# Second mixer of a two-layer diffusion backbone: copies shared out anew, the residual loaded late, and identity products on TensorE while the accumulators are loaded

## The reference, cut to what matters

```
u  = modulate(rms_norm(x), shift, scale)           # latents and context, 64 groups of 16 features
for d in (forward, backward):
    h[t] = lam_bar * h[t-1] + b_bar @ u[t]         # 64 complex states per group; context first, then latents
    y   += real(c_mat @ h)
z  = gelu(y + u * d_skip)
x  = x + gate * (val * sigmoid(gt)),   [val, gt] = z @ glu_w + glu_b
```

## Time and profile before

| what | us |
|---|---|
| median of three runs | 2512.29 (2508.5 to 2512.55) |
| the profiled execution, its time | 2506.16 |
| its span in the trace | 2504.4 |
| PE busy | 2143.6 (86% of the span) |
| DVE busy | 1092.3 (44%) |
| ACT busy | 509.8 (20%) |
| `s5_mixer`, from its first DMA to its last addition | 1461.3 to 1759.3 |

### The profile page before, as it was taken

How to read it: one execution, slowest core, us unless ns; L and a number is a source line. 1 busy time by engine, 2 the same in 40 slices (tenths; PEclk the granted TensorE clock), 3 DMA queues, 4 the chain that set the end, 5 groups by cost and what they waited for, 6 DMA issues and landing times. The chain is left out here.

```text
span 2504.4 us, 40476 instructions
## 1 busy us (share of the span) xinstructions
PE 2143.6 (86%) x11989; PEld 1189.9 (48%) x11990; DVE 1092.3 (44%) x2311; ACT 509.8 (20%) x945; POOL 433.9 (17%) x359
## 2 busy tenths in 40 slices
PE   5889999997999999999999816699789999988874
PEld 3765444744544444444444405354444444444442
DVE  8853365944543333333333338942532222222222
ACT  3443233611121111111111125220221111100000
POOL 1000000002012222222222210000122222232332
PEclk9999999998999999999999968799799999999997
DMA  9971002003799999999999669830499999899996
GB/s 358 386 265 46 34 34 84 1 1 131 264 346 355 354 358 357 359 351 350 355 358 358 202 158 329 275 146 0 160 404 375 361 363 358 274 390 372 385 385 207
DMA packets 173622, 666.72 MB, mean 266 GB/s; under 512 B 37666, under 2 KB 48898, under 8 KB 129882
## 3 DMA queue, kind: packets, MB, share of 16 engines
q1 hardware_dynamic: 121410, 564.71, 58.7%
q0 software_dynamic: 36160, 64.84, 11.0%
q10 hardware_dynamic: 15960, 35.96, 4.1%
HBM read 617.29 MB, written 86.09 MB: 281 GB/s over the span
## 5 line engine op out<-in xcount | busy, mean ns | idle before, releaser
L1518 PE MATMUL banks_l<-slotw_l,xTw_l 128*128 128x512 f32 x800 | 358.2, 601 | 27.7 <-issue 27.7
L1529 PE MATMUL banks_l<-slotn_l,xTn_l 128*64 128x256 f32 x2816 | 325.0, 383 | 34.5 <-issue 34.5
L1529 PEld LDWEIGHTS banks_l<-slotn_l,xTn_l 128*64 128x64 f32 x2816 | 212.0, 137 | 178.9 <-issue 104.8
L1518 PEld LDWEIGHTS banks_l<-slotw_l,xTw_l 128*128 128x128 f32 x800 | 148.5, 191 | 239.3 <-issue 239.3
L1568 PE MATMUL banks_l<-slotn_l,late_l 128*64 128x512 f32 x704 | 189.9, 615 | 19.6 <-DVE late_l L1356 17.9
L1547 PE MATMUL banks_l<-slotw_l,late_l 128*128 128x512 f32 x400 | 191.8, 602 | 15.4 <-DVE late_l L1338 15.4
L977 POOL DMA_INDIRECT xgw_l<-moe_h,idxw_l x58 | 60.6, 1045 | 741.0 <-PE banks_l L1463 367.1
L1005 POOL DMA_INDIRECT moe_acc<-late_l,idxn_l x88 | 151.2, 1718 | 190.5 <-DMA moe_acc<-late_l,idxn_l 172.5
L937 POOL IOTA slotw_l<- 128x1 f32 x2 | 0.3, 140 | 729.1 <-POOLq L69 431.3
L1335 DVE TENSOR_TENSOR late_l<-late_l,banks_l 128x256 f32<-128x256 f32 x50 | 21.0, 421 | 240.2 <-ACT late_l L1107 240.2
L556 PE MATMUL ps_a<-W_a,hT_a 128*128 128x512 f32 x288 | 124.9, 595 | 0.0
(11 more groups left out here) (433 smaller groups left out, 3235.0 us busy)
## 6 DMA issues: line engine op xcount, KB each, us to landing
slotn_l<-in_exp_w_gate SPq DMA_DIRECT2D x88, 1024.0 KB
slotn_l<-in_exp_w_up SPq DMA_DIRECT2D x88, 1024.0 KB
slotn_l<-in_exp_w_down SPq DMA_DIRECT2D x88, 1024.0 KB, 12.1
slotw_l<-in_exp_w_gate SPq DMA_DIRECT2D x50, 1024.0 KB
slotw_l<-in_exp_w_up SPq DMA_DIRECT2D x50, 1024.0 KB
slotw_l<-in_exp_w_down SPq DMA_DIRECT2D x50, 1024.0 KB
w_p<-in_mod_w SPq DMA_DIRECT2D x12, 2048.0 KB, 15.4
W_a<-in_ar_w_in SPq DMA_DIRECT2D x5, 2048.0 KB, 9.4
```

The source lines that it names most:

```text
L1518: last = pe.matmul(pGU_w, xT_w[b % 2][:, k, :], wgu[0][b % WIDE_RING][:, :, k, :], start=(k == 0), stop=(k == KD - 1))
L1529: last = pe.matmul(pGU_n[H * side:H * side + H, b % 2], xT_n[b % 2][:, k % 4, H * (k // 4):H * (k // 4) + H], w[:, :, k, P * side:P * side ...
```

## The change

- ACT issues the loads of `vec` ahead of all its others.
- PE multiplies the identity by itself 90 times (128 x 128, into the bank 6 that nobody reads) after it has transposed the modulation vectors (L2452) and before it waits for `Xn`.
- The eight copies of the residual go. `x` is loaded from the first accumulator and `XR` (the lower half of `XS`) from the second, by eight DMAs each, late: the first between the GLU's bias and the second half of its weights, the second when the last product of the output stage is done. DVE adds them behind the first GLU tile.
- So SP issues the factors of half-blocks 4 to 6 at once. ACT issues the first modulation weight when `Xn` is complete, the next two after uT. The weights' buffers are rotated, and output factors 3 and 4 wait for m5 instead of m7.
- DVE makes its copy in half-blocks 2, 5, 8, 11 and 14 only, ahead of the sweep of the block that they belong to; ACT makes it in the other eleven. Sweeps are no longer interleaved with copies by thirds: `sweep(0)` follows half-block 1. PE's wait ahead of t0 counts all copies, as before.
- 57 memsets for 50.

```diff
-        w = [v.rearrange("p (k n) -> p k n", k=HK) for v in (ZU[:, 0], ZU[:, 1], XS[:, SG * NCL:])]
+        w = [v.rearrange("p (k n) -> p k n", k=HK) for v in (XS[:, SG * NCL:], ZU[:, 0], ZU[:, 1])]
+        XR = XS[:, 0:NL * D].rearrange("p (m d) -> p m d", m=NL)
...
-        XN_DVE, R_ACT = 5, 2
+        XN_DVE, R_ACT, WARM = 5, 2, 90
+        DVE_CTX = (2, 5, 8, 11, 14)
+        def evicted(hb):
+            return 3 * (hb + 1) - ctx_copied(hb)
+        def ctx_copied(hb):
+            return sum(k <= hb for k in DVE_CTX)
...
             for hb in range(R_ACT, NHB):
-                if hb == 4:
-                    sp.wait_ge(S['x_sum'], SL)
-                    for m in range(NL):
-                        for hh in range(2):
-                            sp.dma_start(x[hh * 64:hh * 64 + 64, m, :], X[0:64, 2 * m + hh, :]).then_inc(S['xres_in'], 16)
...
-            sp.wait_ge(S['mod_mm'], LATE)
+            sp.wait_ge(S['mod_mm'], LATE - 2)
...
+            for m in range(NL):
+                for hh in range(2):
+                    sp.dma_start(x[hh * 64:hh * 64 + 64, m, :], tile_rows(parts[0], m, hh)).then_inc(S['xres_in'], 16)
             glu_half(1)
+            sp.wait_ge(S['o_mm'], NB)
+            for m in range(NL):
+                for hh in range(2):
+                    sp.dma_start(XR[hh * 64:hh * 64 + 64, m, :], tile_rows(parts[1], m, hh)).then_inc(S['xres_in'], 16)
...
         def _(act):
+            [the three loads of vec, moved here from behind the loop]
             for j in range(2):
...
+            act.wait_ge(S['xn_done'], XN_DVE)
+            act.wait_ge(S['xn_act'], SL - XN_DVE)
+            act.dma_start(w[0], mod_weights(io, *MOD_LATE[0], 0)).then_inc(m_in[0], 16)
...
-            act.wait_ge(S['xres_in'], 16 * 8)
-            for n in range(3):
+            for n in range(1, 3):
                 act.dma_start(w[n], mod_weights(io, *MOD_LATE[n // 2], n % 2)).then_inc(m_in[n], 16)
...
+                if hb not in DVE_CTX:
+                    act.activation(VH[64:P, 0:NCC, :, gs].rearrange("p c a g -> p g a c"), v_of(hb)[64:P, :, :, 0:NCC], ACT.Copy)\
+                       .then_inc(S['va_done'], 1)
...
-            dve.wait_ge(S['xres_in'], 16 * 8)
-            for hb in range(NHB):
-                dve.wait_ge(S['va_done'], 2 * hb + 1)
-                dve.tensor_copy(VH[64:P, 0:NCC, ...], v_of(hb)[64:P, :, :, 0:NCC]).then_inc(S['vd_done'], 1)
-                if 2 <= hb < 14:
-                    b, third = divmod(hb - 2, 3)
-                    sweep(b, third)
-                    if third == 2:
-                        sweep(b, 3)
-            for b in range(4, NB):
+            dve.wait_ge(S['xn_act'], SL - XN_DVE)
+            for b in range(NB):
+                for hb in (2 * b, 2 * b + 1):
+                    if hb in DVE_CTX:
+                        dve.wait_ge(S['va_done'], evicted(hb - 1) + 1)
+                        dve.tensor_copy(VH[64:P, 0:NCC, ...], v_of(hb)[64:P, :, :, 0:NCC]).then_inc(S['vd_done'], 1)
                 for stage in range(4):
                     sweep(b, stage)
...
-            for _ in range(50):
+            for _ in range(57):
...
+                if u == 0:
+                    dve.wait_ge(S['xres_in'], 16 * 16)
+                    for t in range(NL):
+                        done(dve.tensor_tensor(x[:, t, :], x[:, t, :], XR[:, t, :], ALU.add))
+                    done.wait()
                 done(dve.tensor_tensor(x[:, m, c], x[:, m, c], a, ALU.add))
...
             last.then_inc(S['vec_mm'], 1)
+            for _ in range(WARM):
+                pe.matmul(ps[:, 6 * 512:6 * 512 + P], ident[:], ident[:], start=True, stop=True)
             pe.wait_ge(S['xn_done'], XN_DVE)
...
-            pe.wait_ge(S['va_done'], 2 * NHB)
-            pe.wait_ge(S['vd_done'], NHB)
+            pe.wait_ge(S['va_done'], evicted(NHB - 1))
+            pe.wait_ge(S['vd_done'], ctx_copied(NHB - 1))
```

More of the change, by code:

```diff
@@ L2087, in s5_mixer, with tile_rows @@
         NPAIR, NFILL = NCK // 2 - 1, NCL // 2
-        XN_DVE, R_ACT = 5, 2
+        XN_DVE, R_ACT, WARM = 5, 2, 90
[4 more added lines that the diff above has]
+            return sum(k <= hb for k in DVE_CTX)
+        def tile_rows(part, m, hh):
+            return part.rearrange("(m h c) d -> m h c d", m=NL, h=2)[m, hh, 0:NCL, :]
         CTX_OPS, STEPS = 4 * 4, NCL // 2 - 1
@@ L2178, in _ @@
         def _(act):
+            for s in range(2):
+                act.dma_start(vec[:, 2 * s:2 * s + 2], io['modrow'][1, s, 0:2 * D].rearrange("(a g j) -> g a j", a=2, j=SI)).then_inc(S['vec_in'], 16)
+            act.dma_start(vec[:, 4], io['norm1_g'][1].rearrange("(g j) -> g j", j=SI)).then_inc(S['vec_in'], 16)
             for j in range(2):
@@ L2181, in _ @@
                    .then_inc(x_in[j], 16)
-            for s in range(2):
-                act.dma_start(vec[:, 2 * s:2 * s + 2], io['modrow'][1, s, 0:2 * D].rearrange("(a g j) -> g a j", a=2, j=SI)).then_inc(S['vec_in'], 16)
-            act.dma_start(vec[:, 4], io['norm1_g'][1].rearrange("(g j) -> g j", j=SI)).then_inc(S['vec_in'], 16)
             act.dma_start(lam[:, 0].rearrange("p a b g -> p (a b g)"), io['s5_l8']).then_inc(S['l8_in'], 16)
@@ L2334, in sweep @@
                         dve.wait_ge(S['up'], n)
-                    dve.wait_ge(S['va_done'], 4 * (b + 1))
-                    dve.wait_ge(S['vd_done'], 2 * (b + 1))
+                    dve.wait_ge(S['va_done'], evicted(2 * b + 1))
+                    if ctx_copied(2 * b + 1):
+                        dve.wait_ge(S['vd_done'], ctx_copied(2 * b + 1))
                     dve.tensor_tensor(a, even, factor(0, 0, NPAIR, g), ALU.mult).then_inc(S['up'], 1)
@@ L2345, in sweep @@
                     dve.tensor_tensor(odd, a, c[:, :, ::-1, :], ALU.add).then_inc(S['up'], 1)
-            dve.wait_ge(S['xres_in'], 16 * 8)
-            for hb in range(NHB):
-                dve.wait_ge(S['va_done'], 2 * hb + 1)
-                dve.tensor_copy(VH[64:P, 0:NCC, :, 4 * hb:4 * hb + 4].rearrange("p c a g -> p g a c"), v_of(hb)[64:P, :, :, 0:NCC])\
-                   .then_inc(S['vd_done'], 1)
-                if 2 <= hb < 14:
-                    b, third = divmod(hb - 2, 3)
-                    sweep(b, third)
-                    if third == 2:
-                        sweep(b, 3)
-            for b in range(4, NB):
+            dve.wait_ge(S['xn_act'], SL - XN_DVE)
[3 more added lines that the diff above has]
+                        dve.wait_ge(S['va_done'], evicted(hb - 1) + 1)
+                        dve.tensor_copy(VH[64:P, 0:NCC, :, 4 * hb:4 * hb + 4].rearrange("p c a g -> p g a c"), v_of(hb)[64:P, :, :, 0:NCC])\
+                           .then_inc(S['vd_done'], 1)
                 for stage in range(4):
@@ L2472, in _ @@
                 if hb >= 4:
-                    pe.wait_ge(S['va_done'], 2 * (hb - 3))
-                    pe.wait_ge(S['vd_done'], hb - 3)
+                    pe.wait_ge(S['va_done'], evicted(hb - 4))
+                    if ctx_copied(hb - 4):
+                        pe.wait_ge(S['vd_done'], ctx_copied(hb - 4))
                 for g in range(4):
```

## The result

The change costs a quarter of a per cent. In 20 runs of each kernel the median after is 2512.18 us (2508.0 to 2524.86), before 2505.24 (2501.54 to 2516.3); the ratio is 1.0026 with a 95% interval of 1.0015 to 1.0037. The kernel before measured 7 lower over these 20 runs than in the first three of them, so the forecast of 2510.0 lies close to 2512.18 by its number, yet its sign is wrong: a gain of 2.3 was forecast, a loss of about 6.9 was measured.

A forecast was written before the change was run, and what follows sets the result against it. DVE's recurrence and the queue of weights and tables bound the mixer side by side, DVE's path longer by 2.8 us. First GLU product 2.3 earlier: 2506.16 - 2.3 = 2503.9 profiled, 2510.0 against the median; range 2503.0 to 2516.0.

The forecast's parts named there:

- the slack between m7 and the fill: Before the first fill, DVE was ready 2.8 us after m7 ended; afterwards the fill would wait for m7, not DVE.
- the start: Mixer's start up to V: X1's last part shares the engines with factors 4 to 6; last `sums` some 0.6 late.
- the estimate of equal turns: X1's last part at the start: queues served in equal turns would give a landing at up to 1497.2.
- X1's first part is issued 2 us later, so `sums(0)` about 1472.4: Start, loads of `vec` moved ahead: `sums(0)` about 1472.4, and PE starts the 90 products at 1476.9.
- It costs nothing: PE's 90 products ahead of uT: the block ends at 1498.9 to 1501.0, before `Xn` at 1502.0.
- copies and sweeps: During and after V: first sweep at T + 7.4, sweeps end at T + 39.9, saving DVE 7.6 us.
- ACT needs about 1.7 a half-block: ACT's copies in V: about 1.7 a half-block, 3.4 a block, so DVE stays the slower.
- I take 7.0: it lands at 1564.1: Weights' chain: weight 3, in an empty queue, takes 7.0 and lands at 1564.1 against 1564.8; m7 ends at 1602.9.
- the output stage: First fill to GLU: fill 3.4 earlier, block 5 only 0.7, first GLU product 2.3 earlier, within 0.7 to 3.4.
- The rival in which DVE's path decides: First fill: starts when DVE is ready, 1598.0, GLU 8.4 earlier at 1637.2; 2503.9; chance 28%.
- the GLU: GLU stage: loads of x and XR and four additions of 1.2 on DVE are hidden; nothing taken, 4.9 if uncovered.
- 7 more memsets, 0.9 us, lie ahead of the first tile [...] I take nothing.: DVE ahead of the first GLU tile: 7 more memsets, 0.9 us, are hidden and cost nothing.

The follow-up runs named there:

- held factors: Kernel after, but SP holds factors 4 to 6 until the last `sums`, as before; 2512.0 us, ratio 1.0025 against the kernel before.
- old copies: Kernel after, but DVE makes all 16 small copies, with sweeps interleaved by thirds as before; 2508.75 us, ratio 1.0002.
- factors first: Kernel after, but output factors 5 to 7 are issued ahead of the GLU's bias and first half of its weights; 2512.16 us, ratio 1.0005.
- the old ones: Kernel after with factors 4 to 6 held, copies and sweeps in the old order, and 46 memsets; 2508.57 us, ratio 1.0002.
- tables first: Kernel after, but SP issues table n-1 ahead of the wait for m(n-3) and weight n; 2517.04 us, ratio 1.0032.

## Why the prediction was wrong, by its steps

The GLU begins 8.5 later from the mixer's start. By the table of marks: V +3.6; t0 behind V +3.5; t0 and m0 at the lower clock +2.1; the chain from m0 to m7 -1.1; the slack between m7 and the fill -2.6; from the fill to the GLU +3.0. The forecast had, in this order, -0.8, +3.2, +2.4, -5.5, -2.7, +1.1. The first, fourth and last are wrong. The first and last had been taken towards the favourable end of their bounds, the fourth in the middle of its own (7.0 between 5.4 and 8.4). Together they make up 10.7 of the 10.8 between forecast and marks.

- **Failed: the start.** "Shared, it lands at 1489.2 + 4.9 = 1494.1, and `sums` starts some 0.6 late." It is 4.2 late by the marks; the bound was 4.0. The step took the third part's 4.9 us as the price of sharing, but SP's queue was running dry then; with 1.5 MB more behind it X1 shares to the end. The kernel with held factors shows this cause: there the last `sums` is back at 32.8. Here the estimate of equal turns, worked out from the round robin by packets of the Trainium skill ("DMA: Bandwidth & Descriptors", "Queues, rings and completion order"), which I set aside, was nearly right: a landing at 1497.2 is 35.9 in the marks' terms, and the last part landed at 1469.6 + 32.1 - 1465.34 = 36.4.
- **Failed: "X1's first part is issued 2 us later, so `sums(0)` about 1472.4".** It began at 18.5, not 11.1: issued behind the vectors, the first part took 16.3 to land. By itself that costs the last `sums` little (32.8 with held factors, for 32.3), but PE's products stand behind `sums(0)`, and so "It costs nothing" fell with it. Their length was right (22.6 for 22.0 to 24.1), the place wasn't (they began at 22.7 for 15.6); the 1.3 they bring is right too.
- **Right in the main: copies and sweeps.** First sweep 7.3 after V (7.4), sweeps' end at V + 40.1 (39.9), t0 at V + 36.5 (36.2), t0 and m0 5.4 (5.7), with the clock at 0.50 until 1564 and m0's end at 1565.5. The reading that t0 would fall behind DVE's copy of 14 was the change's centre, and with old copies it is back at V + 32.5. What was mis-sized is ACT: "ACT needs about 1.7 a half-block" was 1.92, since a half-block with three copies takes it 2.15 to 2.20 and one with two some 1.34: the third adds over 0.8, not 0.45. DVE stayed the slower, so t0 was not hurt by this, but about half of the delay stays when DVE's copy no longer is the last.
- **Failed: "I take 7.0: it lands at 1564.1".** Weight 3 took 9.7, above even the 8.4 of weight 0. The queue was empty, and the step took that for more of a gain than it was: of the 17 kernels five had 11.8 to 12.5 here, the one before among them, and twelve 8.9 to 10.1, none 7.0. Why a weight in an empty queue takes that long stays open. In the whole chain the loss of 2.7 at the landing and 1.6 behind it (36.9 for 35.3) turned 45.8 from m0's end to m7's end into 50.2. It had been 51.3: a chain whose length behind its first weight is nearly fixed moves with its start, and t0's start was what the change delayed.
- **Failed: the output stage.** "Three blocks are left in which PE [...] catches up with the fills." PE did not: factor 5 came 3.0 late, and 42.2 passed from the fill to the GLU for 39.2. The factors' loads moved with m7, as the step said, but the step then took a value towards its upper bound. The wait of 2.7 to 4.5 appears in every kernel in which m7 holds the fill and the factors stand in the old order; factors first removes it.
- **Right: DVE doesn't decide.** The fill follows m7 directly, DVE having been idle for 9.2. The rival in which DVE's path decides fell.
- **Right: the GLU.** The loads and the four additions are hidden; PE is busy for 20.00 of 20.00 beside them.
- **Right by number only: "7 more memsets, 0.9 us, lie ahead of the first tile [...] I take nothing."** They cost nothing there, but with the 50 of before the second MoE takes some 40 us more. The step asked what they cost and not what they are for.

That the loss of time hangs on the copies in the main is shown by pairs of kernels: factors held with the new copies 1.0025, with the old ones 1.0002, whose intervals only touch at 1.0011. How much of it they carry is not settled: added alone to the kernel before they cost its mixer 2.8 to 3.1, taken out of the kernel after they give 6.9, of which 1.5 is a V that happened to come earlier. That the start and the factor wait carry the rest rests on the marks of single executions; factors first has a ratio of 1.0005 with an interval up to 1.002, and held factors did not move it.

## What to carry to other kernels

When work is shared out anew to relieve one engine, look first at whose first product waits for its last copy: a chain whose length is set by transfers starts there and moves as a whole, so relief elsewhere ends in a wait. Idle time ahead of a transfer is not spare bandwidth for a later one to be issued early beside it; price sharing by the case in which the other queue stays full to the end. And when an edit takes instructions off an engine, look at every later stage of that engine too, not at the stage that was edited alone.

## What the runs showed of the hardware that was not expected

- **The number of DVE instructions ahead of a later loop can change that loop's time.** 2300 and 2304 instructions: second MoE 775.1 and 779.8, 78 and 79 instruction packets. 2310, 2311 and 2322: 738 to 746, 36 or 37 packets. In two pairs of kernels the memsets alone differ. That the loop's code then has to be fetched again in its passes is the likely reading of the packets and of DVE's pauses of up to 10.3 us; the runs show the count, the packets and the pauses, not the mechanism.
- **A small load in front delays the large one behind it.** Three loads of 4 to 8 KB landed 5.9, 9.0 and 10.5 us after their issue, and the first part of X1 behind them 16.3 after its own. The first `sums` began 16.8 to 20.0 after the mixer's first DMA in all ten kernels with these loads in front, and 9.1 to 9.2 in all seven with them behind.
- **Ending a run of products doesn't keep the clock for the stage after next.** The clock was at 1.00 until 1516 and at 0.50 from 1517, with PE partly busy on the rounds of uT. V began low in both kernels.
- **Tables lower the rate.** In five stretches of 4 us in which the queue moved them (two before, one after, two with tables first) the engines' share was 1.13 to 1.16 at 217 to 284 GB/s, against some 370 to 420 at shares of 0.97 to 1.03 with factors or weights.
- **A third small copy costs ACT more than the spacing of two shows.** A half-block with one copy of 128x512 and one of 64x256 took ACT some 1.34 us, one with two of 64x256 2.15 to 2.20; the second of 64x256 was estimated at 0.45 and adds over 0.8. Eleven of them turned an engine with pauses into one without.
